# Even layer's first gates, second queries and keys as three products of halves; modulation steps in the first attention; PSUM banks set by place

## The reference

```python
h, gate = _modulate(x, c, norm_g, w_ada, b_ada)          # rmsnorm(x) * (1 + scale) + shift
hc, gate_c = _modulate(xc, c_ctx[None, :], norm_g, w_ada, b_ada)
qa, ka, va, qb, kb, vb, g = _split(h @ w_in, EVEN_SPLITS)    # likewise for hc
ya = _window_gqa_sink(qa, ka, va, kac, vac, a_sink)          # first attention, 8 heads of 64
yb = _diff_attend(qb, kb_all, vb_all, lam)                   # second attention, 4 x 2 heads of 64
y = concatenate([ya, rmsnorm(yb)]) * silu(g)
x = x + gate * (y @ w_out)
```

## Time and profile before

| | |
|---|---|
| median of 3 runs | 2316.11 us |
| the profiled execution, its own time | 2317.48 us |
| its span | 2315.7 us |
| mean granted TensorE clock | 0.998 |
| TensorE busy (matmul) | 2266.7 us, 98% of the span |
| VectorE, ScalarE, GpSimd busy | 1306.6, 795.1, 326.6 us |
| first attention, by TensorE's work | about 103 to 232 us of the span |
| qb, kb, vb (proj B) | 232 to 372 us |

### The profile page before, as it was taken

The page is one execution under the profiler, slowest core; times in us unless marked ns, Lnnn a source line. Parts: engine busy times, 40 slices in busy tenths (PEclk is TensorE's granted clock), DMA queues, the critical chain, the costliest instruction groups (busy, mean ns, idle before and its releaser), DMA issues.

```text
span 2315.7 us, 30849 instructions
## 1 busy us (share of the span) xinstructions
PE 2266.7 (98%) x11976; PEld 1727.6 (75%) x11976; DVE 1306.6 (56%) x2919; ACT 795.1 (34%) x1707; POOL 326.6 (14%) x349
## 2 busy tenths in 40 slices
PE   7999999999999999999999999999999999999998
PEld 5866577678546667788876888887878678888886
DVE  3565565754246544758768476665368845443334
ACT  4245102531012203723558132223443643222233
POOL 2200110001000111021100110003543001000154
PEclk9999999999999999999999999999999999999999
DMA  7200331002234373023310245554222103322322
GB/s 314 74 19 19 122 115 64 19 19 64 96 118 128 94 218 99 5 70 107 106 41 2 94 163 185 193 186 142 96 96 73 38 1 118 128 100 94 107 93 80
DMA packets 58270, 225.92 MB, mean 98 GB/s; under 512 B 20478, under 2 KB 21118, under 8 KB 41740
## 3 DMA queue, kind: packets, MB, share of 16 engines
q1 hardware_dynamic: 58124, 223.94, 28.9%
HBM read 221.83 MB, written 2.10 MB: 97 GB/s over the span
## 4 chain that ended last, share of the span: by engine, by line
PE 90%; DVE 4%; POOL 2%; ACT 1%; DMA 1%; issue 1%; SPq 1%; POOLq 0%; ACTq 0%; DVEq 0%
PE PS L86 85%; PE PS L91 5%; POOL WKr L103 1%; DMA GB<-in_ev_ada 1%; DVE WK L108 1%; SPq L162 1%; DVE WK L142 1%; ACT WK L98 1%; ACT WKr L96 0%; DVE SM L135 0%; POOL SM L103 0%; DVE WK L115 0%; ACT WK L96 0%; DVE X L115 0%; DMA RING<-in_l_qi 0%
## 5 line engine op out<-in xcount | busy, mean ns | idle before, releaser
L86 PE MATMUL PS<-Hr,GBr 128*128 128x512 f32 (+1 forms) x1332 | 440.8, 384 | 0.0
L86 PE MATMUL PS<-Hr,RINGr 128*128 128x512 f32 (+1 forms) x1112 | 410.1, 373 | 0.0
L96 ACT ACTIVATE WK<-PS 128x512 f32<-128x512 f32 (+2 forms) x391 | 189.0, 516 | 453.9 <-PE PS L86 276.0
L86 PE MATMUL PS<-H,RING 128*128 128x512 f32 (+1 forms) x928 | 336.4, 515 | 2.7 <-DVE GB L115 2.7
L115 DVE SCALAR_TENSOR_TENSOR ACC<-ADA,SM,ACC 128x256 f32<-128x256 f32 x608 | 291.7, 502 | 40.0 <-DMA ADA<-in_l_mod 21.4
L86 PEld LDWEIGHTS PS<-Hr,GBr 128*128 128x128 f32 x1332 | 247.7, 188 | 51.4 <-issue 3.9
L86 PEld LDWEIGHTS PS<-H,RING 128*128 128x128 f32 x928 | 172.1, 190 | 139.4 <-issue 128.9
L103 DVE TENSOR_TENSOR RINGr<-RING,GBr 128x1024 fp32r<-128x1024 f32 x148 | 183.6, 1278 | 138.3 <-ACT GBr L96 137.8
L86 PE MATMUL PS<-RING,GB 128*128 128x256 f32 x1152 | 251.2, 379 | 0.0
L86 PEld LDWEIGHTS PS<-RING,GB 128*128 128x128 f32 x1152 | 218.1, 190 | 30.4 <-issue 1.3
L86 PEld LDWEIGHTS PS<-Hr,RINGr 128*128 128x128 f32 x1112 | 208.8, 188 | 37.8
(11 more groups left out here) (222 smaller groups left out, 2825.3 us busy)
## 6 DMA issues: line engine op xcount, KB each, us to landing
ADA<-in_l_mod SPq DMA_DIRECT2D x96, 512.0 KB, 3.7
RING<-in_l_gu SPq DMA_DIRECT2D x44, 1024.0 KB, 4.9
RING<-in_l_wd SPq DMA_DIRECT2D x24, 1024.0 KB, 4.9
RING<-in_ev_in SPq DMA_DIRECT2D x13, 1024.0 KB, 5.7
ADA<-in_od_ada SPq DMA_DIRECT2D x24, 512.0 KB, 3.6
RING<-in_od_in SPq DMA_DIRECT2D x11, 1024.0 KB, 6.2
RING<-in_l_in SPq DMA_DIRECT2D x10, 1024.0 KB, 5.0
RING<-in_l_out SPq DMA_DIRECT2D x8, 1024.0 KB, 4.9
```

What stands on the lines that cost most here:

```text
L86: self.last = self.eng.matmul(out, lhsT, rhs, start=start, stop=stop, skip_group_check=True)
L96: self.last = self.eng.activation(out, in_, func, bias=bias, scale=scale)
```

## The change

- `_is_split` takes chunks 0 to 8 in place of 0 to 2: the gates of t = 0 to 3, qb and kb become three products of halves. `hi_place` names places for the rounded halves of chunks 3, 4, 5 and 7 in the gates' later space and beside the attention's buffers, which move closer together (`P_at`, `PT_at`).
- ScalarE rounds chunks 3, 4 and 5 in turns 2, 4 and 16 of the first attention, and 6, 7 and 8 ahead of qb 0, qb 2 and kb 0. GpSimd subtracts after each.
- The whole activations are made after the last tile of kb, since they overwrite the halves: k = 0 and 1 on VectorE, 2 to 7 on GpSimd. VectorE's rope of kb 2 moves behind them.
- `values_by_feature` makes the first half of vb with k in the outer loop over all six row tiles, two tiles to a bank.
- Six modulation steps (one each) go into turns 3, 5, 10, 11, 17 and 20 of the first attention. After the tiles of qb and kb there are 3 steps (2 after kb 2 and kb 3) in place of 4. From vb on the cursor stands 2 to 4 steps further than before, until the end of the fourth attention.
- `banks_from(b)` sets the bank counter at six places of TensorE's program, of which the end of `attention` serves all of them.

```diff
 def _is_split(i):
-    return PLAN[i][0] in SPLIT or PLAN[i][0] == "ev_in" and PLAN[i][1] < 3
+    return PLAN[i][0] in SPLIT or i < 9
...
-STEP_TURNS = {"M": range(18)}
+STEP_TURNS = {"A": (3, 5, 10, 11, 17, 20), "M": range(18)}
...
+ROPE_STEPS = {(tag, t): 2 if tag == "kb" and t > 1 else 3 for tag in ("qb", "kb") for t in range(4)}
...
+            elif i == 4:
+                place = WKr[:, 6656:7680] if h else GBr[:, 5120:6144]
+            elif i in (3, 5, 7):
+                place = GBr[:, 3072 + h * 1024:4096 + h * 1024]
...
+            def banks_from(b):
+
+                turn["set"], turn["at"] = list(range(8)), b - 1
...
+            def values_by_feature(i, tag):
...
+                for k in range(8):
+                    wait_h("whole", k, 0)
+                    for t in range(6):
+                        at = t % 2 * 256
+                        pe.matmul(bank(where["p", tag, t, 0], at, at + 256), Ht(k, t * 128, (t + 1) * 128), W[:, k, :],
+                                  k == 0 and t % 2 == 0, k == 7)
...
+                    if t < 4:
+                        (Wh, Wl), c = split_weights(i, 8), slice(t % 2 * 128, t % 2 * 128 + 128)
+                        pe.wait_ge(rest_signal(i), ("rest", i, k // 4))
+                        wait_h("ev", k, part // 4)
+                        hh, hl = Hh("ev", k, s0, s0 + n), Hl("ev", k, s0, s0 + n)
+                        pe.matmul(bank(7, 0, n), Wh(k, c), hh, k == 0, False)
+                        pe.matmul(bank(7, 0, n), Wh(k, c), hl, False, False)
+                        pe.matmul(bank(7, 0, n), Wl(k, c), hh, False, k == 7)
+                        continue
...
-                        fm(i, 8, m, tag, t, roped(tag, t), ALLT, Ht, whole, rotate)
-                        ada(4)
+                        fm_split("ev", i, m, tag, t, roped(tag, t), ALLT, rotate)
+                        ada(ROPE_STEPS[tag, t])
                     chunk_done(i)
...
+            values_by_feature(9, ("vb", 0))
+            ada(4)
+            chunk_done(9)
+            banks_from(2)
+            tm(10, 8, 0, 256, ("vb", 1), lambda t: copied(("vb", 1), t, 0), range(6), Ht, whole)
...
+                for ahead in {2: (3,), 4: (4,), 16: (5,)}.get(i, ()):
+                    round_chunk(ahead)
...
+                    if t % 2 == 0 and q * 2 + t // 2 < 3:
+                        round_chunk(6 + q * 2 + t // 2)
...
-                for k in {2: (0, 1), 3: (2, 3, 4), 4: (5, 6, 7)}.get(i, ()):
-                    dve.wait_ge(pe_product, ("p", "va", VA_TILES[-1], 0))
-                    dve.tensor_tensor(Ht(k), Hh("ev", k, 0, 768), Hl("ev", k, 0, 768), ALU.add)
-                    dve.then_inc(dve_value, ("whole", k))
...
+                    if tag == "kb" and t == 3:
+                        dve.wait_ge(pe_product, ("p", "kb", 3, 512))
+                        for k in range(2):
+                            dve.tensor_tensor(Ht(k), Hh("ev", k, 0, 768), Hl("ev", k, 0, 768), ALU.add)
+                            dve.then_inc(dve_value, ("whole", k))
...
+            for k in range(2, 8):
+                own()
+                pool.wait_ge(pe_product, ("p", "kb", 3, 512))
+                pool.tensor_tensor(Ht(k), Hh("ev", k, 0, 768), Hl("ev", k, 0, 768), ALU.add)
+                pool.then_inc(pool_value, ("whole", k))
```

More of the change, by code:

```diff
@@ L830, in program, with whole_signal @@
         gates_t, wi_t = WK[0:24, 5120:5632], WK[0:8, 6656:7040]
+        def whole_signal(k):
+            return dve_value if k < 2 else pool_value
         def product(tag, t, s0, n):
+            if tag == ("vb", 0):
+                return bank(where["p", tag, t, s0], t % 2 * 256, t % 2 * 256 + n)
             return bank(where["p", tag, t, s0], 0, n)
@@ L927, in wait_h @@
                 elif st == "whole":
-                    pe.wait_ge(dve_value, ("whole", k))
+                    pe.wait_ge(whole_signal(k), ("whole", k))
                 else:
@@ L1011, in tm @@
                     pe.then_inc(pe_product, ("p", tag, t, 0))
+            def values_by_feature(i, tag):
+                W = ring_view(i, 8)
+                pe.wait_ge(ring_in[i % NRING], ("ring", i))
+                for t in range(0, 6, 2):
+                    where["p", tag, t + 1, 0] = next_bank(("p", tag, t, 0), copied(tag, t, 0) + copied(tag, t + 1, 0))
+                for k in range(8):
[4 more added lines that the diff above has]
+                                  k == 0 and t % 2 == 0, k == 7)
+                for t in range(6):
+                    pe_product.at["p", tag, t, 0] = pe_product.n + 1
+                pe.then_inc(pe_product)
             def copied(tag, t, s0):
@@ L1075, in products @@
                     pe.wait_ge(act_value, ("pt", tag, u, U["of"][i]))
-                    pe.matmul(O, V, PT_at(u, i, 0, 128)[0:kw, :], U["first"] and h not in begun,
+                    pe.matmul(O, V, PT_at(tag, u, i, 0, 128)[0:kw, :], U["first"] and h not in begun,
                               U["last"] and i == by[h][-1])
@@ L1117, in attention @@
                         behind(i)
-                turn["set"] = list(range(8))
+                banks_from(0)
             def sum_squares(key, srcs, n, by):
@@ L1297, in tensor @@
             first_turned(7)
-            turn["set"] = list(range(8))
+            banks_from(7)
             close(of_pe, "norm ev")
@@ L1430, in tensor @@
             for j in range(2):
+                if j:
+                    banks_from(5)
                 gates_m(FIRST["od_in2"] + 1 + j, 4 + 2 * j)
@@ L1770, in rope @@
                 act.then_inc(act_value, ("raw", tag, t))
+                if (tag, t) == ("kb", 3):
+                    act.wait_ge(dve_value, ("whole", 1))
                 for s0, n in segs[1:]:
@@ L2684, in vector, with values_a @@
                 copy_out("va", t, 0, 128)
[L2686 removed]
+            def values_a(i):
                 for t in VA_AT.get(i, ()):
                     copy_out("va", t, 0, 128)
[L2689 to L2694 removed]
+            cur.allowed |= {"ev"}
+            attention("A", None, values_a)
             close(of_dve, "att A")
             since(dve, "att A")
[L2699 removed]
             for tag in ("qb", "kb"):
                 for t in range(4):
[L2702 to L2703 removed]
+                    if tag == "kb" and t == 3:
[3 more added lines that the diff above has]
+                            dve.then_inc(dve_value, ("whole", k))
+                        own(("whole", 1))
+                        rope("kb", 2, ALLT)
+                    if (tag, t) != ("kb", 2):
+                        rope(tag, t, ALLT)
+                    ada(ROPE_STEPS[tag, t])
             for j in range(2):
@@ L3194, in gpsimd @@
             since(pool, "proj A")
+            cur.allowed |= {"ev"}
+            rest(3)
+            rest(4)
+            for turn in STEP_TURNS["A"]:
+                if turn == 17:
+                    rest(5)
+                ada(1)
             close(of_pool, "att A")
             since(pool, "att A")
-            cur.allowed |= {"ev"}
-            for tag in ("qb", "kb"):
+            for q, tag in enumerate(("qb", "kb")):
                 for t in range(4):
+                    if t % 2 == 0 and q * 2 + t // 2 < 3:
+                        rest(6 + q * 2 + t // 2)
                     rope(tag, t)
-                    ada(4)
+                    ada(ROPE_STEPS[tag, t])
+            for k in range(2, 8):
[3 more added lines that the diff above has]
+                pool.then_inc(pool_value, ("whole", k))
             ada(4)
@@ L3458, in sync @@
             load()
-            for j in range(2):
-                load()
             cur.allowed |= {"ev"}
-            for j in range(4):
-                ada(4)
-                ada(4)
-                load()
+            for turn in STEP_TURNS["A"]:
+                if turn == 17:
+                    load()
+                ada(1)
+            load()
+            for tag in ("qb", "kb"):
+                for t in range(4):
+                    ada(ROPE_STEPS[tag, t])
+                    if t % 2:
+                        load()
             ada(4)
```

37 lines of the change are left out of this document (17 added, 20 removed).

## The result

| | before | with the change |
|---|---|---|
| median | 2316.82 us (9 runs) | 2321.31 us (9 runs, 2319.55 to 2324.2) |
| ratio | | 1.0024 (95% interval 1.0016 to 1.0032) |
| span of the profiled execution | 2315.7 us | 2319.5 us |
| mean granted clock | 0.998 | 0.993 |

What follows compares the result with a forecast made beforehand. TensorE, busy 98% of the span, was taken as the bound. Gains of 27.5 us less costs of 13.7 gave 13.8 off the profiled 2317.48, 2303.7, or 2302.3 us for the median; range 2289.5 to 2309.5.

Steps and rivals of the forecast that it cites:

- Gains, 27.5 us: Shorter TensorE work: second queries and keys 15.8 us, first gates 9.1, whole activations out of the attention 2.6.
- third and fourth lines of the ledger: Forecast gains by stretch: first attention with qb 0, 5.5 us; qb 1 to the end of vb, 8.4 us.
- Applies after qb 2 and kb 0, 6.2 us: Proj B: GpSimd's subtractions delay VectorE's modulation, so TensorE waits some 3 us at each place; 6.2 us, between 0 and 10.
- Whole sums ahead of vb, 1.0 us: After kb 3: GpSimd's sums may start first and delay VectorE's k = 0; 1.0 us, between 0.2 and 3.
- Subtractions in the attention, 3.5 us: Turns 4, 5, 16 and 17: GpSimd's subtractions stop VectorE's weighing; 2.0 plus 1.5 us, between 0 and 9.8.
- steps there, 1.5: Modulation steps in turns 5, 10, 11 and 17 overrun the small turns' VectorE idle time; 1.5 us, between 0 and 4.
- Roundings, 1.5 us: First attention: three ScalarE roundings each delay a copy of turned blocks by about 0.5 us; 1.5 us, between 0 and 6.
- VectorE bounds the queries and keys: Rival: stops never overlap VectorE's idle, costing 3.4 us a pair of tiles, 10.2 for three; 2309.8 us, chance 0.15.
- The slower case: Rival: every subtraction and sum on GpSimd becomes TensorE's wait, 41 us, 13.6 over the gain; 2329.7 us, chance 0.04.
- Nothing comes of it: Rival: weight reads, shifted steps and banks give the gain back in out projection and odd layer's start; 2314, chance 0.04.
- all of it is hidden: Rival: GpSimd runs only where VectorE idles, so costs fall to about 1 us; 2289.6 us, chance 0.15.

Runs made afterwards that it cites:

- e8: The change with the three mends of e1, e2 and e5 together: 2290.26 us, ratio 0.9881 to the kernel before.
- e1: The change with vb's first half starting at bank 3 and its second at bank 0: 2314.78 us, ratio 0.9989 to the kernel before.
- e5: The change with chunks 4 and 5 subtracted on VectorE, in turns 5 and 22, in place of GpSimd: 2316.69 us, ratio 0.9996.
- e2: The change with the subtractions of chunks 6, 7 and 8 on VectorE, ahead of the ropes, in place of GpSimd: 2307.33 us, ratio 0.9962.
- e10: e8 with chunks 4 and 5 subtracted by GpSimd again, but later, rounded in turns 7 and 22: 2293.6 us, ratio 0.9896 to the kernel before.
- e3: The change with up to 4 modulation steps after each tile from qb 0 to kb 1 in place of 3: 2314.35 us, ratio 0.9987.
- e6: The change with four unused float32 filling products on TensorE before its wait at the applies after qb 2 and kb 0: 2317.61 us, ratio 0.9998.
- e9: e8 with 18 modulation steps after the tiles of qb and kb in place of 22: 2294.25 us, ratio 0.9904 to the kernel before.
- e11: e8 with no modulation step in the first attention and up to 4 after every qb and kb tile: 2300.19 us, ratio 0.9925.
- e12: e9 with vb's first half starting at bank 6 and its second half at bank 1: 2286.21 us, ratio 0.987 to the kernel before.

## Why the prediction was wrong

- **Gains, 27.5 us: right.** Tiles take 9.20 us as forecast. Gate parts are 1.56 and 1.63 us for the forecast 1.48 and 1.54 (in e8, 153.13 to 154.69 and 139.02 to 140.65), some 1.5 us over all parts. The waits of turns 3 and 4 went. In e8, which changes only who subtracts, when, and the banks, the third and fourth lines of the ledger hold 24.7 us of the 27.5.
- **Applies after qb 2 and kb 0, 6.2 us: the wait right, its price wrong.** 3.97 us each against "some 3"; none after kb 2, as forecast. The step that failed is that a wait was priced at its length. The clock adds 3.3 us to each: 14.5 us in all, 8.3 of the fourth line's 17.2. The clock of 1.00 in the earlier trace rows is that of stretches in which nothing waits; the one place of the trace of before that shows the price, 49.33 us, was not read.
- **Whole sums ahead of vb, 1.0 us: the wrong cause.** The sums cost 0.3 (e1). Banks cost 9.0, which is 8.0 of the 17.2: the copy of kb 2, moved behind the sums, held one (5.31), ScalarE's copies of vb's first half another (1.39), and 2.3 are clock. The step that failed is the reading of who is queued behind the moved rope: it asked who wants its result and not who wants its bank. "The shifted cursor and the banks change who waits for whom later on; I allow 1 us either way" is the sentence that covered both this loss and the gain of 3.7.
- **Subtractions in the attention, 3.5 us, and steps there, 1.5.** The waits are 3.45 and 1.87 us, with the clock behind them about 6.5 (e5), inside the bounds of 0 to 9.8. The steps of modulation showed no cost of their own.
- **Roundings, 1.5 us:** 0.17 and 0.48 us of waits for ScalarE, of which 0.25 were there before; nearly nothing.
- **A row misread, without effect.** Of the two long instructions of the earlier trace rows only the one of 2622 ns stood behind a subtraction. The weighing of 2576 ns is at 922.60 us, beside a GpSimd product of 128x960 (2.43 us from 922.33).
- **The rivals.** "VectorE bounds the queries and keys" had the wait nearly to size (3.4 a pair) and not the clock. The slower case had the right engine, but priced it by GpSimd's busy time. "Nothing comes of it" has the nearest time, 2314, by a loss in the later stages that measured 1.0 us; of the waits that made the time it says nothing. e8 looks like "all of it is hidden", 2289.6 forecast and 2290.26 measured, but that close a hit is in part luck: the 3.7 us ahead of qa 0 were in no sum, and they cover the 2.8 us by which the gains fell short.

Open: what exactly starts a fall. After the waits of 3.45 us and more it fell each time that nothing filled them. After shorter ones it fell in some profiled executions and not in others: after 1.87 us in turn 17 in five of seven, after 2.3 us at some 1040 us in three of ten (the change, e2, e8), after 1.82 in one of two, not after the 1.03 and 1.62 of the earlier trace rows nor after the 1.44 and 1.88 of e10. Where the apply's 16 products of one column stand right behind the wait it fell after 1.70 and 1.14 us (e3) and after 0.53 (e6), but not after 0.50 (e6, kb 0) nor without a wait (e2, e8).

The later stages are settled in part. From the wait of 0.87 us to the end are 1925.1 to 1925.7 us in the three runs whose steps stand from vb on as before (e9, e11, e12), 1928.6 to 1931.7 in the ten whose steps stand further on, and 1928.7 in the kernel before. So the steps' place costs some 3 us and more there. TensorE's waits for VectorE's weighing (L108) add up to 4.9 to 5.3 us in the three, 5.4 before, 6.6 in the change and 7.6 in e8; the largest, at 1047 us, is 2.33 us in the change for 0.90. Against it stands a gain that nobody forecast: the waits for VectorE's L115 on `GB` are 1.9 us in all of these runs for 4.2 before. What took them away was not tried.

## What to carry to other kernels

Price a wait of TensorE as its length and, from about 1 us on, the half clock that may follow it, and look in the trace of before for one place that shows that price. When a step is moved behind another, ask which PSUM banks it empties and who takes them next, as well as who reads its result. Work that GpSimd takes over is free only where VectorE has nothing due: here the same subtraction cost 1.2 us on VectorE, and on GpSimd it stopped VectorE for up to 2.4.
